# Inverse roots by exp and ln, sums of squares in two fp32r passes, and five attention steps placed anew in a hybrid decoder step

## The reference, cut to what matters

```python
def rmsnorm(x, g):
    xf = x.astype(jnp.float32)
    y = xf * lax.rsqrt(jnp.mean(xf * xf, axis=-1, keepdims=True) + EPS)
    return (y * g.astype(jnp.float32)).astype(x.dtype)

def layer(x, pos, s_ret, s_gla, conv_prev, ln1, w_in, ...):
    n = rmsnorm(x, ln1)
    rq, rk, rv, rg, gq, gk, gv, gg, ga, m_r, m_g = split_cols(n @ w_in)
    ...
    o_r, s_ret_new = chunked_gated_linear(rq, rk, rv, log_g, s_ret)
    y_r = (group_rmsnorm(o_r, g_ret) * jax.nn.silu(rg)) @ w_ret_out
    z = (ga @ w_gate_up + b_gate_up).astype(jnp.float32)
    log_a = (jax.nn.log_sigmoid(z) / GLA_GATE_TAU).reshape(B, L, GLA_HEADS, GLA_DK)
    ...
    o_g, s_gla_new = chunked_gated_linear(gq, gk, gv, log_a, s_gla)
    y_g = (group_rmsnorm(o_g, g_gla) * jax.nn.silu(gg)) @ w_gla_out
    mix = jax.nn.sigmoid(m_r) * y_r + jax.nn.sigmoid(m_g) * y_g
    h = x + mix @ w_o
    n2 = rmsnorm(h, ln2)
    ...
```

## Time and profile before

| | |
|---|---|
| runs shown | 830.57 us median of 3 (830.27 to 831.93) |
| profiled execution, own time | 831.75 us |
| its span, first to last instruction | 829.0 us |
| TensorE matmuls busy | 816.5 us, 6544 instructions |
| VectorE busy | 588.6 us |
| ScalarE busy | 374.9 us |
| GpSimd busy | 217.2 us |
| granted TensorE clock, mean | 0.997 of full speed |

### The profile page before, as it was taken

The page is one execution under the profiler, slowest core; times in us unless marked ns, Lnnn a source line. Parts: engine busy times, 40 slices in busy tenths (PEclk is TensorE's granted clock), DMA queues, the critical chain, the costliest instruction groups (busy, mean ns, idle before and its releaser), DMA issues.

```text
span 829.0 us, 15746 instructions
## 1 busy us (share of the span) xinstructions
PE 816.5 (98%) x6544; PEld 804.8 (97%) x6544; DVE 588.6 (71%) x765; ACT 374.9 (45%) x524; POOL 217.2 (26%) x258
## 2 busy tenths in 40 slices
PE   9999999999999999999999999999999999999996
PEld 8989999999999999999999999999999999999996
DVE  5455668577898886766558877777777756878973
ACT  5544234232354554534343544444434424544574
POOL 4008246544325500000430333333223322000020
PEclk9999999999999999999999999999999999999998
DMA  9768977983325974538897587477687873765622
GB/s 271 215 203 137 243 248 183 201 244 123 109 97 107 202 255 140 174 96 272 174 272 220 104 262 219 139 201 185 245 211 203 229 165 97 202 182 170 176 65 108
DMA packets 163025, 152.27 MB, mean 184 GB/s; under 512 B 6677, under 2 KB 144617, under 8 KB 162940
## 3 DMA queue, kind: packets, MB, share of 16 engines
q1 hardware_dynamic: 129420, 109.73, 42.5%
q0 software_dynamic: 33376, 41.04, 26.4%
q10 hardware_dynamic: 160, 0.53, 0.2%
HBM read 145.31 MB, written 58.40 MB: 246 GB/s over the span
## 4 chain that ended last, share of the span: by engine, by line
PE 94%; DVE 3%; issue 1%; DMA 1%; SPq 0%; ACT 0%; DVEq 0%
PE mm L2036 51%; PE ax L2333 14%; PE mm L2447 8%; PE ax L2055 6%; PE ax L2447 6%; PE mm L2333 4%; PE ax L2060 2%; PE mm L2117 1%; DVE grs L1455 1%; DMA x_nat<-in_x_prompt 1%; PE mm L2048 0%; DVE ylo L1703 0%; DVE wlo L1715 0%; DVE wlo L1445 0%; PE mm L2055 0%
## 5 line engine op out<-in xcount | busy, mean ns | idle before, releaser
L2036 PE MATMUL mm<-nhi,whi 128*128 128x272 f32 x928 | 196.2, 293 | 0.0
L2036 PE MATMUL mm<-nhi,wlo 128*128 128x272 f32 x928 | 191.9, 288 | 0.0
L2036 PE MATMUL mm<-nlo,whi 128*128 128x272 f32 x928 | 191.4, 288 | 0.0
L1021 ACT ACTIVATE whi<-raw 128x1024 fp32r<-128x1024 f32 (+3 forms) x112 | 128.5, 1181 | 68.7 <-PE mm L2036 38.5
L2036 PEld LDWEIGHTS mm<-nhi,whi 128*128 128x128 f32 x928 | 146.2, 188 | 2.9 <-issue 1.1
L2036 PEld LDWEIGHTS mm<-nlo,whi 128*128 128x128 f32 x928 | 145.8, 188 | 0.0
L2036 PEld LDWEIGHTS mm<-nhi,wlo 128*128 128x128 f32 x928 | 145.0, 189 | 0.0
L1715 DVE TENSOR_TENSOR wlo<-raw,whi 128x1024 fp32r<-128x1024 f32 (+1 forms) x78 | 84.4, 1123 | 5.7 <-ACT whi L1021 3.2
L1445 DVE TENSOR_TENSOR wlo<-raw,whi 128x2048 fp32r<-128x2048 f32 x27 | 65.2, 2414 | 15.3 <-ACT whi L1021 15.3
L952 POOL DMA_DIRECT2D v_sums<-in_w_up x24 | 30.7, 4231 | 117.4 <-DVE mlo L1786 117.1
L1021 ACT ACTIVATE whi<-ring 128x1408 fp32r<-128x1408 f32 x25 | 34.6, 1383 | 44.1 <-PE ax L2447 24.0
(11 more groups left out here) (390 smaller groups left out, 1983.8 us busy)
## 6 DMA issues: line engine op xcount, KB each, us to landing
raw<-in_w_in SPq DMA_DIRECT2D x36, 512.0 KB, 5.0
raw<-in_w_up SPq DMA_DIRECT2D x36, 512.0 KB, 7.1
ring<-w_sums SPq DMA_DIRECT2D x16, 704.0 KB, 4.9
w_sums<-in_w_down SPq DMA_DIRECT2D x9, 768.0 KB, 9.8
w_sums<-in_w_down POOLq DMA_DIRECT2D x9, 768.0 KB, 10.0
ring<-in_w_down SPq DMA_DIRECT2D x9, 704.0 KB, 4.5
v_sums<-in_w_up SPq DMA_DIRECT2D x24, 256.0 KB, 7.5
v_sums<-in_w_up POOLq DMA_DIRECT2D x24, 256.0 KB, 14.3
```

The costliest lines, as they stand in the source:

```text
L1021: return act.activation(out, in_, func, **kw).then_inc(done, 1)
L2036: ins = pe.matmul(mm[:, 2 * j + a, 0:HALF], w, x[:, kx, HALF * a:HALF * (a + 1)], start=first and n == 0 and m == 0, stop=last and n == le ...
```

## The change

The two whole norms and the eight head norms take x to the power -1/2 as exp(-ln(x)/2) on ScalarE; VectorE's reciprocal goes. For a head norm ScalarE writes the square twice, once rounded to fp32r (`gsq_high`) and once in full; VectorE subtracts the two into `gsq_low` in fp32r; TensorE sums both with fp32r ones. In `ORDER`: `za` and `z` go before the second half of unit 3, `zs` and `la` to block 2 of it; `gn 1` goes before `v 6`; `v 7` to block 2 of (11, 1); `rs 3` and `rp 3` to blocks 1 and 2 of (14, 1), behind `y2 2`, `y2 3`, `y1 4`. The wait on `o_ready` goes from the root to the square.

```diff
@@ middle_order
-        (1, 0): [("vec",)], (1, 1): [("cache",)], (2, 1): [("sc",)], (3, 1): [("la",), ("v", 0)],
+        (1, 0): [("vec",)], (1, 1): [("cache",)], (2, 1): [("sc",)], (3, 0): [("z",)], (3, 1): [("v", 0)],
...
-        (10, 1): [("v", 6), ("gn", 1), ("gsq", 2)],
-        (11, 0): [("v", 7)],
+        (10, 1): [("gn", 1), ("v", 6), ("gsq", 2)],
...
-        (14, 0): [("rs", 3), ("rp", 3), ("y2", 2), ("y2", 3), ("y1", 4)],
+        (14, 0): [("y2", 2), ("y2", 3), ("y1", 4)],
...
-        (3, 1): {2: [("za",)], 4: [("z",)], 6: [("zs",)]},
+        (3, 0): {6: [("za",)]}, (3, 1): {2: [("zs",), ("la",)]},
...
-        (11, 1): {4: [("ro", 0)]}, (12, 0): {4: [("gn", 2), ("rk", 1), ("gsq", 3), ("gi", 2)]},
+        (11, 1): {2: [("v", 7)], 4: [("ro", 0)]}, (12, 0): {4: [("gn", 2), ("rk", 1), ("gsq", 3), ("gi", 2)]},
...
-        (14, 1): {4: [("rn", 2), ("ro", 3), ("ri", 2)], 6: [("rx", 3), ("rw", 3), ("rsq", 3), ("y1", 5), ("y2", 4)]},
+        (14, 1): {1: [("rs", 3)], 2: [("rp", 3)], 4: [("rn", 2), ("ro", 3), ("ri", 2)], 6: [("rx", 3), ("rw", 3), ("rsq", 3), ("y1", 5), ("y2", 4)]},
@@ ScalarE
-        def root(name, width):
+        def inverse_root(name, width):
 
             aux_wait_filled(act, name)
-            run(halves(rstd[:, :]), bank2(name), ACT.Sqrt, drained_sem(name), scale=1.0 / width, bias=eps)
+            run(halves(rstd[:, :]), bank2(name), ACT.Ln, drained_sem(name), scale=1.0 / width, bias=eps)
+            aux_wait_drained(act, name)
+            run(rstd[:, :], rstd[:, :], ACT.Exp, rstd_ready, scale=-0.5)
...
+                if n == 0:
+                    st.did(act.activation(ones_r[:, :], ones, ACT.Copy))
+                if n > 1:
+                    act.wait_ge(o_ready, n - 1)
+                st.did(act.activation(gsq_high[n][:, :], normed(NORMS[n]), ACT.Square))
                 run(gsq[:, :], normed(NORMS[n]), ACT.Square, osq_done)
             elif k in ("gn", "rn"):
                 aux_wait_filled(act, s)
-                if norms > 1:
-                    act.wait_ge(o_ready, norms - 1)
-                run(halves(grs2[norms % 2][:, :]), bank2(s), ACT.Sqrt, drained_sem(s), scale=1.0 / DV, bias=eps)
+                run(halves(grs2[norms % 2][:, :]), bank2(s), ACT.Ln, drained_sem(s), scale=1.0 / DV, bias=eps)
+                aux_wait_drained(act, s)
+                run(grs2[norms % 2][:, :], grs2[norms % 2][:, :], ACT.Exp, root_ready, scale=-0.5)
                 norms += 1
@@ VectorE
-        def inverse(out, name, done):
-            aux_wait_drained(dve, name)
-            dve.reciprocal(out, out).then_inc(done, 1)
...
+            elif k in ("gsq", "rsq"):
+                n = NORMS.index(("gn" if k == "gsq" else "rn", s[1]))
+                dve.wait_ge(osq_done, n + 1)
+                dve.tensor_tensor(gsq_low[:, :], gsq[:, :], gsq_high[n][:, :].bitcast(F32), ALU.subtract).then_inc(osq_low, 1)
             elif k in ("gi", "ri"):
                 s = ("gn" if k == "gi" else "rn", s[1])
                 root = grs2[norms % 2]
-                inverse(root[:, :], s, dve_step)
-                st.n += 1
-                st.wait()
+                dve.wait_ge(root_ready, norms + 1)
@@ TensorE
+        def summed_parts(name, high, low):
+
+            aux_take(pe, name)
+            for a in range(2):
+                t = HALVES[a]
+                small(bank(name, a)[:, 0:HALF], ones_r[:, :], high[:, t], stop=False)
+                small(bank(name, a)[:, 0:HALF], ones_r[:, :], low[:, t], start=False, done=filled_sem(name) if a else None)
...
             elif k in ("gn", "rn"):
-                pe.wait_ge(osq_done, NORMS.index(s) + 1)
-                summed(s, gsq)
+                pe.wait_ge(osq_low, NORMS.index(s) + 1)
+                summed_parts(s, gsq_high[NORMS.index(s)], gsq_low)
```

More of the change, by code:

```diff
@@ L307, in build @@
     grs2 = [grs, at("grs1", [P, NT], C + 11 * T)]
+    gsq_low = at("gsq_low", [P, NT], o_rope, F32R)
+    high_at = [at(f"gsq_high{i}", [P, NT], off, F32R) for i, off in enumerate((o_rope + T, g - T, C + 11 * T))]
+    gsq_high = [high_at[n % 2 if n < 7 else 2] for n in range(2 * HEADS)]
     o += 2 * T
@@ L381, in build @@
     ones = c1[:, C1_ONE:C1_ONE + P]
+    ones_r = at("ones_r", [P, P], a0 + 2 * KD * T + C1_ONE * 4, F32R)
     eps = c1[:, C1_EPS:C1_EPS + 1]
@@ L431, in build @@
     sq_done, acc_done = sem("sq_done"), sem("acc_done")
-    rstd_ready = sem("rstd_ready")
+    rstd_ready, root_ready = sem("rstd_ready"), sem("root_ready")
     last_sq, last_sums, last_roots, last_rstd = map(sem, ("last_sq", "last_sums", "last_roots", "last_rstd"))
@@ L442, in build @@
     k3_high, k3_ready = sem("k3_high"), sem("k3_ready")
-    osq_done, o_ready = sem("osq_done"), sem("o_ready")
+    osq_done, osq_low, o_ready = sem("osq_done"), sem("osq_low"), sem("o_ready")
     swapped, qk_ready = sem("swapped"), sem("qk_ready")
@@ L1093, in _ @@
             elif k == "rstd1":
-                root("rstd1", D_MODEL)
+                inverse_root("rstd1", D_MODEL)
             elif k == "v":
@@ L1290, in _ @@
             hi(u + 2, u % 2, 32 * (u // 2 + 2), (filled[1], FW[1] + n + 1))
-        root("rstd2", D_MODEL)
+        inverse_root("rstd2", D_MODEL)
         for i in range(KF // 2):
@@ L1518, in _ @@
             elif k == "rstd1":
-                inverse(rstd[:, :], "rstd1", rstd_ready)
                 dve.wait_ge(rstd_ready, 1)
@@ L1831, in _ @@
             lo(u + 2, u % 2, u + 3)
-        inverse(rstd[:, :], "rstd2", rstd_ready)
+        aux_wait_drained(dve, "rstd2")
         dve.memset(ext[:, 0:2], 0.0).then_inc(conv_done, 1)
@@ L2074, in summed @@
             for a in range(2):
-                small(bank(name, a)[:, 0:HALF], ones, sq[:, HALF * a:HALF * (a + 1)],
+                small(bank(name, a)[:, 0:HALF], ones if name == "rstd1" else ones_r[:, :].bitcast(F32), sq[:, HALF * a:HALF * (a + 1)],
                       done=filled_sem(name) if a else None)
+        def summed_parts(name, high, low):
[4 more added lines that the diff above has]
+                small(bank(name, a)[:, 0:HALF], ones_r[:, :], low[:, t], start=False, done=filled_sem(name) if a else None)
         def keep_busy(n):
@@ L2481, in sums @@
             for j in (2 * e, 2 * e + 1):
-                small(mm[:, e, j:j + 1], sq[:, P * j:P * (j + 1)], ones[:, 0:1], start=start and j == 2 * e, stop=stop,
+                small(mm[:, e, j:j + 1], sq[:, P * j:P * (j + 1)], ones_r[:, 0:1].bitcast(F32), start=start and j == 2 * e, stop=stop,
                       done=last_sums if e == 0 and j == 1 else None)
             if e == 1:
-                small(mm[0:NS, e, NJ:NJ + 1], sq[:, SEQ:NT], ones[:, 0:1], start=False, stop=stop,
+                small(mm[0:NS, e, NJ:NJ + 1], sq[:, SEQ:NT], ones_r[:, 0:1].bitcast(F32), start=False, stop=stop,
                       done=last_sums if stop else None)
```

## The result

The changed kernel takes 834.19 us (median of 16 runs); the kernel before, run beside it, 831.25 (16 runs). The ratio is **1.0022, 95% interval 1.0013 to 1.0032**: 1.8 us slower, just beyond the 0.2% that the prediction took as the least that can be told from no change. The forecast was 829.8, 0.8 us faster. One of the 16 runs after took 990.76 us at a mean granted clock of 0.753; it stands in the median and not in the ratio. The profiled execution after has a span of 832.5 us and an own time of 835.02, against 829.0 and 831.75 before.

What follows compares the result with a forecast made beforehand. TensorE's own stream bounds the kernel, busy 816.5 of 829.0 us. Terms -2.2 - 3.4 - 2.0 + 3.3 + 1.3 + 1.1 + 0.8 + 0.3 + 0.1 = -0.7, taken as -0.8: 830.57 to 829.8 us; range 826.0 to 833.4.

Steps and rivals of the forecast that it cites:

- `gn 3`: Head norm on TensorE: the longer path from `gn 2`, 4.7 us against 3.56 of cover, stalls 1.1; with restart +1.3 us.
- `la` half a unit earlier: Near `v 0`: `z` before unit 3's second half removes TensorE's 2.0 us wait and its restart, -2.2 us.
- The price of the sums: Eight norms on TensorE: four fp32r matmuls at 0.50 us replace fp32 products at 0.92, -3.4 us if nothing waits.
- Rival 4: TensorE's norm sums: fp32r matmuls run no faster than 0.23 us each, +3.4, giving 833.2; chance 0.05.
- Two tables: ScalarE, every norm: `Ln` and `Exp` need two loads, the 1.28 us one before `Exp` not hidden.
- Rival 2: ScalarE's norms: one table serves `Ln` and `Exp`, no load between, about 824 us; chance 0.10.
- `gn 1` and `v 6`: TensorE waits 1.65 us for the pair of `gw 3`, then 1.25 for that of `rk 0`; with two restarts +3.3 us.
- 0.72 for the subtraction: VectorE, eight norms: each subtraction of a 128x544 tile takes 0.72 us, as the evacuation at 178.93.
- rival 3: Subtractions hold VectorE too long; GpSimd stretches of 1.6 at `gn 1`, `rn 1`, `rn 2` add about 4 us: 833.8; chance 0.18.
- `ro 3`: TensorE needs `rp 3` drained, now behind two `y2` and one `y1` on VectorE: 0.6 late, with restart +0.8 us.
- The waits that go: TensorE's old waits of 0.3, 0.4, 0.4 and 0.2 us vanish with restarts and pipeline gaps, 2.0 us saved.
- Rival 1: TensorE's stalls of 6.9 us: VectorE, freed of reciprocals, gives half back, 826.5 us; chance 0.17.

## Why the prediction was wrong

A kernel that was to be 0.8 us faster is 1.8 slower by the ratio, and the 834.19 us lie above the stated range as well. Two terms of the sum were mis-sized: what a wait of TensorE costs, and how long the subtraction takes. The waits at `gn 1`, `v 6`, `gn 3` and `rn 3` came where and nearly as long as they were forecast.

- **`la` half a unit earlier: right.** -2.2 forecast, -2.2 at `v 0`. ScalarE's `Ln` and VectorE's evacuation behind it (at 60.43; I said 59.5) fell under cover.
- **The price of the sums: right.** Four fp32r matmuls take 0.50 (`gn 2`: 0.51 at 200.07). Rival 4 is out.
- **Two tables: right.** A load of 1.28 us stands between `Ln` and `Exp` (24 loads from 36 to 300 us, against 11 before), and the next operation starts 0.01 to 0.02 later. Rival 2 is out as a description of this kernel. It is right as a statement of what the chip can do: with the joint table loaded by name the gain is 3.9 us (0.9953), not the 6.6 of the rival, as `rss`, `rst` and `rn 3` still wait.
- **`gn 1` and `v 6`: waits nearly right, price wrong.** Forecast 1.65 and 1.25, measured 1.8 and 1.0. (The prediction's own places, 175.1 and 173.6, give 1.5 and not 1.65; nothing hangs on it.) The failed step is the one that priced a wait as its length and 0.2 of restart. Two waits so close let the clock fall to the lower level, and the 24 matmuls behind cost 4.53 instead of 3.01: **+1.5 us**, confirmed by filling the gap. Nothing in the attention of before showed it, since the longest wait there, the 2.0 of `la`, stood alone and left the clock at 1.00. Only the tail of that trace did: TensorE has no work from 823 us on, and the clock reads 0.66 to 826 and 0.50 to 829. The sum should have held a bound for it.
- **`gn 3`: right** (wait of 0.8 for 1.1; with `gn 2` the step is +0.5, forecast +0.6). **`rn 3`: right** (0.8 for 0.9; +0.7 both). **Gate unit 16: right** (+0.2 for +0.3).
- **`rn 1` and `rn 2`: wrong; this is rival 3.** The term "0.72 for the subtraction" was mis-sized: 1.96 and 3.00. The place (`rs 2` drained 0.3 us before `rn 1` needs it) and the mechanism stood in the rival; it had 0.18. Of its three stretches the one at `gn 1` did not come (0.73 at 170.56). Here it cost 1.0 at `rn 1`, and at `rn 2` 0.8 through `rkn`, `rks` and `rss`, against the 0.72 on which the forecast rested. The earlier trace rows had it on view: 3.88 for a split beside a spread. It was a row to be read as a rule for every VectorE operation with two inputs in SBUF beside a GpSimd one. GpSimd's queue starts within 1.4 us of the subtraction at both places (227.32 and 242.65, against 227.88 and 244.04). The trace of before even has the price of this shape on VectorE beside `rqd` (205.61 to 206.64) and beside the spread (240.45 to 242.37), for operations that take 0.78 and 0.72 alone:

```profile
205.24 1.99 DVE L1639 SCALAR_TENSOR_TENSOR gqk<-gqk,vecs,grs 128x544 f32<-128x544 f32 x1
...
240.53 2.42 DVE L1703 TENSOR_TENSOR ylo<-ysil,yhi 128x544 fp32r<-128x544 f32 x1
```

- **`ro 3`: a wait of 0.4** instead of 0.6, and that too by the stretch: with GpSimd held back it is gone. **The waits that go**: `s0r` and the old `rks` are gone, `rss` came back at other norms.
- The rest of the sum was right within half a microsecond: the kernel with both terms taken away has the forecast's span of 828.3. That it agrees to the tenth is chance: two executions of one kernel differ by more, and that kernel has the wait at `ro 3` taken away too and starts 0.33 us later than before at the start marker.
- **Rival 1** (half the stalls) is out: the stalls came as worked out. VectorE's 29 us did not shorten them, since its queue waits for ScalarE.

## What to carry to other kernels

Where a new operation is put into a queue, price it at what the same form costs beside the neighbour that will run then, not alone; and price each new wait of TensorE twice, at its length and at what a lower clock adds to the block behind it, above all where two waits stand close together. When a fused change comes out flat, run its parts: here places gained 3.5 us, the roots nothing, and the sums lost 3.0, and much of the loss was in the order of a queue and the choice of a table, which an edit of one to three lines mends (3.2 and 5.7 us by the ratios, each alone). A part that comes out at nothing, as the roots did, can still hide a gain and a loss: compare its list of waits. Two functions that follow each other on ScalarE are worth a look at which table is loaded, since here each got its own although one holds both.

## What the runs showed of the hardware

- Waits of 1.8 and 1.0 us at `gn 1` and `v 6`, and of 0.9 and 1.0 at `s0r` and `rks` with the sums alone, were followed by a fall of the granted clock; a single wait of 2.0 us (`la`, before) and one of 1.1 (`rks`, with `gsq 1` moved) were not. 24 matmuls cost 4.53 and 4.01 us behind the pairs, 3.01 otherwise. How much idle time it takes, and how close together, no run here shows.
- A VectorE operation on two SBUF tensors that meets a GpSimd one runs nearly whole after that one has ended (0.59 of 0.73 us, 2.15 of 2.29): 1.96 and 3.00 for 0.73, 3.88 for 2.29. The other way round GpSimd is held: 4.02 for 1.90 and 2.11 for 1.02. A DMA issue of GpSimd alone did not stretch the subtraction (0.73 at 227.03 with GpSimd held back, 0.72 at 260.95 after).
- A table load takes 1.28 us and the next activation starts 0.01 to 0.02 us later. `Ln` and `Exp` come from different tables unless the joint one is loaded by name; then neither needs one, and both still run (0.69 and 0.66 us).
